# Whole four-byte numbers instead of two rounded halves for the operands of both attention mixers

## What is computed

```python
proj = xn @ w_in                      # [qA|kA|vA|qB|kB|vB]
# mixer A: 8 heads of 64, 2 key/value heads, bands of 128 keys for each chunk of 64 queries
sc = einsum('bcqhgd,bckhd->bchgqk', qc, kb) * HEAD_DIM ** -0.5 + bias
probs = softmax(concat([sc, sink]))[..., :-1]
oA = einsum('bchgqk,bckhd->bcqhgd', probs, vb)
# mixer B: 4 heads with two maps of 64, 8 blocks of 128 queries against all keys up to the block
sc = einsum('bqhmd,bkhmd->bhmqk', q, k) * HEAD_DIM ** -0.5 + bias
pr = softmax(sc); a = pr[:, :, 0] - lam * pr[:, :, 1]
oB = rms_norm(einsum('bhqk,bkhe->bqhe', a, v), subln_g) * (1 - lambda_init)
h = h + concat([oA, oB]) @ w_out
```

## Time and profile before

| what | us |
|---|---|
| three runs | 1228.38, 1230.24, 1231.28 |
| median | 1230.24 |
| span of the profiled execution | 1229.7 |
| PE busy in it | 1197.1 (97%) |
| DVE busy | 867.3 (71%) |
| ACT busy | 517.8 (42%) |
| POOL busy | 250.2 (20%) |

### The profile page before, as it was taken

How to read it: one execution, slowest core, us unless ns; L and a number is a source line. 1 busy time by engine, 2 the same in 40 slices (tenths; PEclk the granted TensorE clock), 3 DMA queues, 4 the chain that set the end, 5 groups by cost and what they waited for, 6 DMA issues and landing times.

```text
span 1229.7 us, 17128 instructions
## 1 busy us (share of the span) xinstructions
PE 1197.1 (97%) x6167; PEld 1001.8 (81%) x6167; DVE 867.3 (71%) x1514; ACT 517.8 (42%) x1045; POOL 250.2 (20%) x291
## 2 busy tenths in 40 slices
PE   8999999999888999999999999999999999999997
PEld 7998887788676888888888888888888888888886
DVE  5433786877886577877787777877777999964443
ACT  4312665565655224433343343343344444733321
POOL 0000000344455122232332323323210000000000
PEclk9999999999899999999999999999999999999999
DMA  7464233111831512242322333233499533620101
GB/s 217 89 90 91 50 89 76 42 40 69 222 139 42 164 52 81 82 128 94 121 87 89 125 103 112 95 94 112 146 345 312 172 95 103 225 75 26 43 35 51
DMA packets 127916, 136.08 MB, mean 111 GB/s; under 512 B 15714, under 2 KB 93274, under 8 KB 127770
## 3 DMA queue, kind: packets, MB, share of 16 engines
q1 hardware_dynamic: 127834, 135.00, 36.1%
HBM read 96.77 MB, written 37.22 MB: 109 GB/s over the span
## 4 chain that ended last, share of the span: by engine, by line
PE 61%; issue 4%; DVE 2%; POOL 1%; ACT 1%; POOLq 0%; DVEq 0%; ACTq 0%
PE ps L1723 60%; PE ps L1729 1%; DVE xs L1474 1%; DVE h L1469 0%; DVE conv L1410 0%; POOL stat L687 0%; ACT xs L796 0%; DVE act_t L1185 0%; POOL stat L706 0%; POOL bias_a L712 0%; POOL more_f L714 0%; PE ps L2118 0%; ACT wbuf L793 0%; POOL o_t L709 0%; DVE h L1688 0%
## 5 line engine op out<-in xcount | busy, mean ns | idle before, releaser
L1723 PE MATMUL ps<-act_t,wbuf 128*128 128x512 f32 x1200 | 280.1, 389 | 0.5 <-DVE a_buf L1499 0.5
L1723 PEld LDWEIGHTS ps<-act_t,wbuf 128*128 128x128 f32 x1200 | 225.2, 188 | 47.5 <-DVE a_buf L1499 0.8
L1723 PE MATMUL ps<-wbuf 128*128 128x512 f32 x912 | 214.8, 390 | 0.0
L1723 PEld LDWEIGHTS ps<-wbuf 128*128 128x128 f32 x912 | 170.6, 188 | 35.1
L1723 PE MATMUL ps<-act_t,wq 128*128 128x512 f32 x624 | 152.2, 396 | 3.6 <-DVE wq L1187 3.0
L1723 PEld LDWEIGHTS ps<-act_t,wq 128*128 128x128 f32 x624 | 114.3, 188 | 30.8 <-issue 7.5
L687 POOL TENSOR_TENSOR stat<-stat 128x1 f32<-128x1 f32 x32 | 17.6, 549 | 420.9 <-DVE stat L1194 420.9
L793 ACT ACTIVATE wbuf<-raw 128x512 fp32r<-128x512 f32 (+1 forms) x107 | 69.0, 646 | 73.9 <-PE ps L1723 63.8
L1723 PE MATMUL ps<-hx,wbuf 128*128 128x512 f32 x408 | 95.7, 389 | 0.0
L1185 DVE TENSOR_TENSOR wbuf<-raw,wbuf 128x512 fp32r<-128x512 f32 (+1 forms) x107 | 87.4, 818 | 11.5 <-ACT wbuf L793 11.2
L1723 PEld LDWEIGHTS ps<-hx,wbuf 128*128 128x128 f32 x408 | 76.5, 188 | 15.9
(11 more groups left out here) (208 smaller groups left out, 1962.8 us busy)
## 6 DMA issues: line engine op xcount, KB each, us to landing
u_ops<-wbuf_f SPq DMA_DIRECT2D x77, 256.0 KB, 2.2
raw<-u_ops SPq DMA_DIRECT2D x77, 256.0 KB, 2.7
raw<-in_w_ffn_in SPq DMA_DIRECT2D x33, 512.0 KB, 3.8
g_ffn<-in_w_ffn_in SPq DMA_DIRECT2D x11, 512.0 KB, 3.9
act_f<-in_w_ffn_out SPq DMA_DIRECT2D x21, 256.0 KB, 4.3
w_raw<-in_w_in SPq DMA_DIRECT2D x10, 512.0 KB, 4.4
wbuf_f<-in_w_ffn_out SPq DMA_DIRECT2D x18, 256.0 KB, 5.9
x_in<-in_x SPq DMA_DIRECT2D x8, 512.0 KB, 3.8
```

The lines of the kernel that those rows point to most:

```text
L1723: return nc.tensor.matmul(dst, lhs, rhs, start=start, stop=stop)
```

## The change

`k_a`, `v_a`, `q_a`, `qk`, `v_b` and `a_t` become plain float32 tiles with one copy each, and the products on them one matmul of type float32 each instead of three (in mixer B's values, instead of two instructions). All `low` and half of the `copy` work on them goes. What goes with it and beside it:

- ACT evicts the units alone (`unit_there`). V is evicted by ACT (three heads) and DVE (fourth head and `v_a`), each once and without waiting for each other.
- `a_t` has two buffers in turn, in both mixers. `mst_a` has its own place and two buffers; mixer A's values now go to partitions 0 to 63 for one key group and 64 to 127 for the other, so its output is 128 x 256 instead of 64 x 512, and its stores and their semaphores follow.
- The order of the loops: in `b_score` the maps are now the outer loop inside a chunk of 512 keys; in mixer A's values the key group is the inner loop.
- Mixer B's output has one part: ACT scales it into `o_t` and squares it right behind, both from PSUM; POOL's add goes. In ACT's order of a step `a_t` now comes ahead of y's half.
- The places of five rows of `w_out` move, and their wait for the last values is at the eighth row instead of the sixth (x == 7 for x == 5).

The split products of the projections, of `mst_a` and of the output projection stay. The core of the diff:

```diff
-                for z, (a, b) in enumerate(SPLIT3):
-                    for m in range(2):
-                        rows = slice(HD * m, HD * m + HD)
-                        at = HALF * (1 + 2 * m)
-                        ins = mm(psf[:, at + kc:at + ke], qk[rows, hb % 2, 0, a, i * P:(i + 1) * P],
-                                 qk[rows, hb % 2, 1, b, kc:ke], z == 0, z == 2)
-                        if ke == w and z == 2:
-                            ins.then_inc(S.b_scores, 1)
+                for m in range(2):
+                    rows = slice(HD * m, HD * m + HD)
+                    at = HALF * (1 + 2 * m)
+                    ins = mm(psf[:, at + kc:at + ke], qk[rows, hb % 2, 0, i * P:(i + 1) * P],
+                             qk[rows, hb % 2, 1, kc:ke], True, True)
+                    if ke == w:
+                        ins.then_inc(S.b_scores, 1)
...
-                    for m, (a, b) in enumerate(SPLIT3):
-                        for g in range(2):
-                            rows = slice(HD * g, HD * g + HD)
-                            ins = mm(ps[:, 1 + 2 * (n % 2) + g, P * c + k0:P * (c + 1)],
-                                     q_a[rows, s, a, ch, :, :].rearrange("p u q -> p (u q)"),
-                                     k_a[rows, b, (ch - 1) * CHUNK + k0:(ch + 1) * CHUNK], m == 0, m == 2)
+                    for g in range(2):
+                        rows = slice(HD * g, HD * g + HD)
+                        ins = mm(ps[:, 1 + 2 * (n % 2) + g, P * c + k0:P * (c + 1)],
+                                 q_a[rows, s, ch, :, :].rearrange("p u q -> p (u q)"),
+                                 k_a[rows, (ch - 1) * CHUNK + k0:(ch + 1) * CHUNK], True, True)
...
-                        for z, (a, b) in enumerate(SPLIT3):
-                            ins = mm(a_out(m, g, c), v_a[kr, vt, a, HD * g:HD * g + HD],
-                                     a_t[kr, b, at:at + P], z == 0, z == 2)
+                        ins = mm(a_out(m, g, c), v_a[kr, vt, HD * g:HD * g + HD], a_t[kr, m % 2, at:at + P],
+                                 True, True)
...
-                    mm(ps[:, 7, 0:2 * P], a_t[:, 0, k * P:(k + 1) * P], v_b[:, k, hb, :], k == 0, False)
-                    ins = mm(ps[:, 7, 0:P], a_t[:, 1, k * P:(k + 1) * P], v_b[:, k, hb, 0:P], False, k == nk - 1)
+                    ins = mm(ps[:, 7, 0:P], a_t[:, m % 2, k * P:(k + 1) * P], v_b[:, k, hb, :], k == 0, k == nk - 1)
...
-                dve.wait_ge(S.b_thi, m + 1)
-                low(a_t[:, 1, 0:w], psf[:, 5 * HALF:5 * HALF + w], a_t[:, 0, 0:w], S.b_tlo)
...
+                m = n - 2
+                w = P * (m % NT + 1)
+                act.wait_ge(S.b_turned, m + 1)
+                if m == 0:
+                    act.wait_ge(S.a_pv, NA)
+                if m >= 2:
+                    act.wait_ge(S.b_pv, m - 1)
+                copy(a_t[:, m % 2, 0:w], psf[:, 5 * HALF:5 * HALF + w], S.b_there)
...
-                col = 4 * (m % 4)
-                nc.scalar.activation(o_sb[:, :, :], ps[:, 7, 0:2 * P].rearrange("p (a q) -> p a q", a=2), ACT.Copy,
-                                     scale=small[:, col:col + 1]).then_inc(S.b_part, 1)
+                r0 = small[:, 4 * (m % 4):4 * (m % 4) + 1]
+                nc.scalar.activation(o_t[:, m % 2, :], ps[:, 7, 0:P], ACT.Copy, scale=r0)
+                nc.scalar.activation(sq_out, ps[:, 7, 0:P], ACT.Square, scale=r0,
+                                     accum_out=stat[:, 16 + 3 * (m % 2):17 + 3 * (m % 2)]).then_inc(S.b_sq, 1)
...
-            nc.gpsimd.tensor_tensor(o, o_sb[:, 0, :], o_sb[:, 1, :], ALU.add).then_inc(S.b_sum, 1)
...
-                if m >= 1:
-                    act.wait_ge(S.a_stored, 32 * m)
-                copy(mst_a[0:HD, 0, :], ps[0:HD, 6 + m % 2, :], S.a_ohi)
+                if m >= 2:
+                    act.wait_ge(a_stored[m % 2], 32 * (m // 2))
+                copy(mst_a[:, m % 2, 0, :], ps[:, 6 + m % 2, 0:2 * P], S.a_ohi)
```

More of the change, by code:

```diff
@@ L513, in _ @@
                 sp.wait_ge(S.a_pv, NA)
-                sp.wait_ge(S.a_stored, 32 * NA)
+                for r in range(2):
+                    sp.wait_ge(a_stored[r], 16 * NA)
                 for j in range(3):
@@ L834, in _ @@
                 act.wait_ge(S.vproj, u + 1)
-                nc.scalar.activation(v_b[:, u, 0:3, 0:P], ps[:, 4 + u % 2, 0:V_CUT].rearrange("p (h n) -> p h n", h=3),
-                                     ACT.Copy)
-                nc.scalar.activation(v_b[:, u, 3, 0:P], ps[:, 6 + u % 2, 0:P], ACT.Copy)
-                copy(v_a[:, u, 0, :], ps[:, 6 + u % 2, P:2 * P], S.vhi)
+                copy(v_b[:, u, 0:3, :], ps[:, 4 + u % 2, 0:V_CUT].rearrange("p (h n) -> p h n", h=3), S.vb_there)
             if t == 2:
@@ L847, in unit_hi @@
             act.wait_ge(S.unit_done, u + 1)
-            copy(tile_dst(j, half, 0), unit_src(u), S.unit_hi, unit_scale(j) or 1.0)
+            copy(tile_dst(j, half), unit_src(u), S.unit_there, unit_scale(j) or 1.0)
         split_w(1)
@@ L906, in _ @@
                 act.wait_ge(S.a_turned, m + 1)
-                copy(a_t[:, 0, 0:HALF], ps[:, 5, :], S.a_thi)
+                copy(a_t[:, m % 2, 0:HALF], ps[:, 5, :], S.a_there)
             if n < NA:
@@ L1253, in _ @@
         nc.vector.tensor_scalar(sinkt[:, 4:8], sinkt[:, 0:4], -1.0, None, ALU.mult).then_inc(S.consts_ready, 1)
-        def unit_lo(u):
-            j, half = u // 2, u % 2
-            dve.wait_ge(S.unit_hi, u + 1)
-            low(tile_dst(j, half, 1), unit_src(u), tile_dst(j, half, 0), S.unit_lo,
-                unit_scale(j))
         split_w(1)
-        for u in range(FIRST_UNITS):
-            unit_lo(u)
-            if u % 2 == 1:
-                split_w((u + 3) // 2)
+        for u in range(1, FIRST_UNITS, 2):
+            split_w((u + 3) // 2)
         next_w = [5]
@@ L1400, in _ @@
             pending_w(n)
-            part = b_fill(n)
-            if part is not None and part % 2 == 1:
-                unit_lo(FIRST_UNITS + part // 2)
             for c in c_units(n):
```

162 lines of the change are left out of this document (70 added, 92 removed).

## The result

| kernel | median us | runs | ratio to before, 95% interval |
|---|---|---|---|
| before | 1229.31 | 1227.64 to 1231.28 | |
| changed | 1215.07 | 1214.85 to 1215.31 | 0.9887 [0.9875, 0.9899] |

The change makes the kernel faster by 14.2 us, 1.1%. The forecast had faster, by 7.2 in its sum (6.3 from this median to its 1223), and its range began at 1215, so the time lies at the very low end of it.

The account below looks back on a forecast made before the run. PE was taken to bound through mixer B step 19, then the longer of PE's work and the score-logits-exp loop. Terms 9.8 - 1.5 - 1.1 - 4.3 - 3.7 - 2.9 - 3.0 - 0.5 = -7.2 us gave 1223, range 1215 to 1255.

Parts of the forecast that it names:

- 9.8: Mixer B scores, steps 0 to 19: longer four-byte score products add 9.8 us of PE time.
- the exp wait: Mixer B, step into w=1024, twice before step 20: PE's 0.72 us idle for the exp goes, -1.5 us.
- the 1.1 for values: Mixer B values: two load-bound 128-column rounds per key block save 0.01 us over 108 blocks, -1.1 us.
- the 3.7 for waits: Up to about 318 us: PE's waits for units' low halves go, since units need only ACT's copy, -3.7 us.
- the clock's -0.5: PE's half clock at 320 to 322 and 388 to 390 us: shorter idle spares some, taken as -0.5 us.
- the rounds of a pair: Score products on two array halves: starts in order, so one pair needs 3 rounds and two pairs 5.
- double round: Mixer B scores: a four-byte round of twice the length, 0.44 us x w/512, not under 0.11.
- loop and tail: Mixer B from step 20 to the output projection: without a_t's low half and with two buffers, -2.9 and -3.0 us.
- Rival (a): Mixer scores and values: four-byte products do not pair across array halves, +22.3 us, 1252; chance 0.32.
- Rival (b): Mixer A values: row pairs but no column pairs, +5.3 us on the forecast, 1228; chance 0.13.
- Rival (c): Four periods instead of three cost nothing and the clock stays up to the end, -12 us, 1218; chance 0.08.
- POOL's add and the late square: Mixer B output: POOL's add goes and ACT's square no longer stands behind the exps; 0 by itself.

Follow-up runs that it names:

- the maps apart: Changed kernel with mixer B's score loop taking all 512-key chunks of map 0 before those of map 1, for over 512 keys; 1215.99 us.
- all three back: Changed kernel with an unread low-half subtraction of a_t on DVE, mixer B's output path as before, and a_t's copy waiting for the previous step's values; 1222.58 us.

## Why the prediction was right and wrong

By stage, both from the two new profiles, whose spans are 15.0 apart:

| stretch | before | after | difference | forecast |
|---|---|---|---|---|
| to the first score of mixer A | 118.19 | 117.39 | -0.8 | 0 |
| mixer A, 16 steps | 78.15 | 72.42 | -5.7 | -4.3 and waits of 0.9 |
| mixer B, steps 0 to 19 | 117.07 | 115.50 | -1.6 | +4.6 |
| steps 20 to 30 | 63.05 | 58.36 | -4.7 | -3.1 |
| score 31 to the output projection | 16.97 | 14.05 | -2.9 | -3.0 |
| from there on | 834.97 | 835.68 | +0.7 | 0 |

(+4.6 is 9.8, less the 1.5 of the exp wait, 0.9 of the 1.1 for values and 2.8 of the 3.7 for waits; the clock's -0.5 had no place.)

**The step that failed: the rounds of a pair.** "Starts are in order, so 0lo waits for 0hi, and 1hi, behind it, starts beside 0lo ... One pair needs 3 rounds, two pairs 5." They are 2 and 4. The price of a double round was right: 0.44 estimated, 0.43 measured. With two rounds the lengths are 1.28 a head over the rounded ones, not 4.2, and for steps 0 to 19 that is 2 x 1.28 + 0.3 = 2.9 where 9.8 stood. This one term is 6.9 us, as much as the whole distance between 7.2 and 14.2; the other deviations are under 1.7 each and cancel in part, by luck (the front -0.8, which is chance, mixer A -0.5, the rest of steps 0 to 19 +0.8, loop and tail -1.5, behind it +0.7). In mixer A the same step failed: scores in 4 rounds instead of 5 are -0.18 a step and not -0.11, while the turns, taken as unchanged, are 0.04 longer. The runs with the maps apart and with the products doubled show what stands in place of the strict order: a pass of one half starts beside a pass of the other that is up to four places ahead of it. What I had taken as the proof of order, rounded products that alternate between the halves, can't tell the two apart, since there the next instruction is always for the free half.

**Rival (a), no pairs,** which had 0.32, falls too. Its mechanism is real (what stands ahead can hold up the other half), but in the doubled run it begins behind four passes, and the change puts two there. The Trainium skill, "TensorEngine Tiling (Array Packing)", Key Properties, says that different tiles load and multiply in parallel; for four-byte operands the trace agrees, with two passes 6 ns apart. **Rival (b)** falls too: mixer A's values take 0.59, where 0.61 was estimated with column pairs and 0.94 without. This and the rest of mixer A's gain are read from the timeline; no run took them back. **Rival (c)** had the nearest time, 1218, and was right in part: in mixer A's passes of 128 columns the periods cost nothing. In mixer B's scores they do cost PE time, 1.28 a head.

**Right as steps.** Mixer A: step 4.59, 4.6 forecast. The values of mixer B got shorter by the 0.01 a block that was taken (eight blocks 1.88 from start to start, 1.96 before), but the turns ahead of them got longer by as much (eight turns 0.87, 0.79 before), so nothing of it is gained; this is the +0.8 of steps 0 to 19. The waits for low halves of units are gone, 0.2 left. The exp wait of 1.5 is gone, but the stated cause (longer scores against a shorter loop) is only one of two: it stays away with short scores and no low half, and with long scores and the low half. Either is enough.

**The loop and the tail.** -5.9 and 0.2 for values were forecast, -7.6 came. The runs take it apart: the low half of a_t alone gives back 4.5 of it, the second buffer 1.4 more once the low half stands behind it (0.5 without), the clock 1.0, and the last unit's low half in step 20 some 0.75, the last by reading alone; 4.5 + 1.4 + 1.0 + 0.75 = 7.65. The 1.0 is seen twice: it is what the turns took off steps 20 to 22 in the kernel before, and what steps 21 and 22 are longer there than with all three back. In the forecast were the first two. That the unit's low half also stands ahead of a difference in DVE's queue I had not followed: I priced it by what PE waited for it. The clock was taken as -0.5; it is 1.0 at the first of its two places and 0.9 to 1.25 at the second.

**Priced at nothing.** POOL's add and the late square: nothing beside the low half, 0.9 alone, though PE's waits for it were 3.3 us. The reason given (the loop sets the time there) holds. That the wait for the row of w_out would grow, from 0 and 0.46 in the two profiles of before to 1.7 and 1.6, was not foreseen. "SP's queue keeps its order" was true, and that was the trouble: the reads are released by the last unit of the output projection's first part, 3.1 us ahead of the first matmul of the rest before (390.36 and 393.43 in the new profile of before) and 1.7 ahead after (375.99 and 377.72). Besides, SP took 2.7 us to come from the first read to the row before and 3.45 after. So the row is issued 0.4 ahead of that matmul before and 1.7 behind it after. Its way from issue to landing differs too (10.6 and 11.7 in the two profiles of before, 10.3 and 10.4 after), and it lands 0.7 to 1.7 later against PE. At the end the stretch is 0.7 longer than before, and 1.4 shorter again with the row between the reads.

## What to carry to other kernels

With 512 columns a product of four-byte numbers takes two passes of 0.43 us where three rounded ones take 0.23 each, and a score of 1024 keys takes 1.92 us instead of 1.59. With 128 columns every pass takes 0.11, and two are cheaper than three: the score of 128 keys takes 0.42 instead of 0.48, mixer A's scores 0.64 instead of 0.82. So the whole numbers pay where the products are narrow, and where they take a low half out of a loop that VectorE sets; they cost where wide products set the time on TensorE. Halves for mixer B's q and k and whole numbers for the rest was the best mix tried here. Products for different halves of the array are to be put no more than four passes apart, which is two four-byte products. When the time on one engine falls, look at the queue of transfers that are issued just ahead of the next stage: they need not get shorter, and their order may begin to matter.

## What the hardware showed that was not expected

- The look ahead of TensorE over the halves of its array: a pass starts beside the one four places ahead of it, in the run with every product twice (four alone at 241.82 to 243.22, in pairs from 243.65), and not before. The first pass of map 1 so starts ahead of three passes of map 0 that stand in front of it.
- The low clock comes and goes between executions of one kernel: the kernel before had it at 320 to 326 and 388 to 390 us in one profile and at 318 to 328 alone in the next. With 24 more turns it was 1.00 at the first place and 0.50 at 386 to 388, and the sum was no gain. Idle time alone doesn't bring it: with all three edits back on the changed kernel PE waits nearly as long around step 20 and at the end, and the clock there is 1.00. But two variants with q and k as halves had it low too, one at 310 to 314 (0.57 and 0.58), one at 392 to 396. What decides it stays open.
- Waits move between names. With y late PE waited 3.2 us for POOL and 2.2 for the exps, without it 0 and 5.4.
